# Hybrid attention and delta-rule layer: 32x32 block inverses by substitution on GpSimd, two chunks at a time

## The reference, cut to what matters

```
lower = jnp.where(strict, jnp.einsum('bhncd,bhnsd->bhncs', k_beta, k) * decay, 0.0)
system = lower + jnp.eye(C, dtype=lower.dtype)
sol = lax.linalg.triangular_solve(system, rhs, left_side=True, lower=True)
a_qk = jnp.where(causal, jnp.einsum('bhncd,bhnsd->bhncs', q, k) * decay, 0.0)
def step(state, inp):
    v_new = u_c - jnp.einsum('bhcd,bhde->bhce', w_c, state)
    o_c = jnp.einsum('bhcd,bhde->bhce', q_c, state) + jnp.einsum('bhcs,bhse->bhce', a_c, v_new)
    state = state * jnp.exp(gl_c)[..., None, None] + jnp.einsum('bhcd,bhce->bhde', kd_c, v_new)
```

## Time and profile before

| what | us |
|---|---|
| median of 3 executions (2544.60 to 2553.95) | 2550.47 |
| the profiled execution | 2535.64 |
| its span | 2533.9 |
| TensorE busy | 2312.9 (91%) |
| VectorE busy | 1082.2 (43%) |
| ScalarE busy | 906.8 (36%) |
| GpSimd busy | 390.6 (15%) |

### The profile page before, as it was taken

How to read it: one execution, slowest core, us unless ns; L and a number is a source line. 1 busy time by engine, 2 the same in 40 slices (tenths; PEclk the granted TensorE clock), 3 DMA queues, 4 the chain that set the end, 5 groups by cost and what they waited for, 6 DMA issues and landing times. The chain is left out here.

```text
span 2533.9 us, 47637 instructions
## 1 busy us (share of the span) xinstructions
PE 2312.9 (91%) x17494; PEld 1329.8 (52%) x17495; DVE 1082.2 (43%) x2488; ACT 906.8 (36%) x2283; POOL 390.6 (15%) x630
## 2 busy tenths in 40 slices
PE   6999999999779999999999997799966999999990
PEld 2545545455356666666666665355534444444440
DVE  2434333343346666666666565133344222222223
ACT  2263462633635555555555544011110010101112
POOL 1000000000111001000000000233221222222224
PEclk9999999999979999999999999899987999999995
DMA  9212121111263213211222103733311879999787
GB/s 335 73 67 76 51 82 44 55 63 36 89 163 106 76 54 95 86 58 63 71 72 80 41 27 155 270 113 129 125 67 50 245 215 309 270 324 301 217 237 290
DMA packets 187895, 334.49 MB, mean 132 GB/s; under 512 B 19723, under 2 KB 119718, under 8 KB 184502
## 3 DMA queue, kind: packets, MB, share of 16 engines
q1 hardware_dynamic: 173878, 281.51, 32.8%
q0 software_dynamic: 13824, 50.34, 8.2%
HBM read 242.36 MB, written 89.44 MB: 131 GB/s over the span
## 5 line engine op out<-in xcount | busy, mean ns | idle before, releaser
L708 PE MATMUL pV<-mod_rows_then_work,w_in_sb 128*128 128x512 f32 x768 | 340.7, 597 | 4.4 <-DMA w_in_sb<-in_w_in_dram 4.4
L2079 PE MATMUL hidden_ps<-w,keys_values_then_all 128*128 x752 | 331.5, 594 | 1.2 <-SPq L1951 1.2
L1147 ACT ACTIVATE probs<-scores,neg_max 128x512 f32<-128x512 f32 (+3 forms) x320 | 199.6, 624 | 332.0 <-DVE neg_max L1276 218.5
L1430 PE MATMUL scores<-keys_values_then_all,queries 96*128 96x512 f32 (+3 forms) x640 | 303.5, 557 | 7.6 <-DMA keys_values_then_all<-kp_d 7.6
L2079 PEld LDWEIGHTS hidden_ps<-w,keys_values_then_all 128*128 128x128 f32 x752 | 143.2, 191 | 181.7 <-issue 181.7
L708 PEld LDWEIGHTS pV<-mod_rows_then_work,w_in_sb 128*128 128x128 f32 x768 | 144.7, 191 | 177.5 <-issue 176.8
L1728 PE MATMUL out_ps<-keys_values_then_all 128*128 128x512 f32 x512 | 226.2, 600 | 2.5 <-ACT keys_values_then_all L1593 2.5
L1435 PE MATMUL bank<-ident,probs 128*128 128x128 f32 x1088 | 183.4, 284 | 1.5 <-ACT probs L1147 1.2
L2009 ACT ACTIVATE keys_values_then_all<-hidden_ps 128x256 f32<-128x256 f32 x47 | 18.0, 384 | 455.7 <-PE hidden_ps L2079 455.7
L1276 DVE TENSOR_REDUCE neg_max<-scores 128x1 f32<-128x512 f32 x192 | 132.2, 688 | 111.5 <-PE scores L1430 110.4
L1447 PE MATMUL outT_ps<-probs_T,keys_values_then_all 128*64 128x128 f32 x2176 | 156.3, 282 | 22.2 <-issue 18.5
(11 more groups left out here) (367 smaller groups left out, 3337.9 us busy)
## 6 DMA issues: line engine op xcount, KB each, us to landing
w<-in_w_dram SPq DMA_DIRECT2D x64, 1024.0 KB, 10.0
w_sb<-in_w_dram SPq DMA_DIRECT2D x32, 1024.0 KB, 14.2
w_mod_rows<-in_w_mod_dram SPq DMA_DIRECT2D x16, 1024.0 KB, 4.8
kqv<-qkv_d SPq DMA_DIRECT2D x16, 768.0 KB, 4.3
mod_rows_then_work<-in_w_mod_dram SPq DMA_DIRECT2D x4, 2048.0 KB, 15.0
x_in<-in_x_dram SPq DMA_DIRECT2D x16, 512.0 KB, 3.5
qkv_d<-l_out SPq DMA_DIRECT2D x32, 256.0 KB, 2.3
keys_values_then_all<-y_d SPq DMA_DIRECT2D x16, 512.0 KB, 5.0
```

The source lines that it names most:

```text
L708: last = pe.matmul(pV[n % 2][:], win[:, k, QKV0 + c * P:QKV0 + (c + 1) * P], hT[:, s % 2, k, :], start=(k == 0), stop=(k == ND - 1))
L1147: act.activation(prob[:, e, 0:w].rearrange("p t k -> p (t k)"), pS[e][:, 0:w * P], ACT.Exp, scale=-1.0, bias=nmin[:, i % 2, h, b:b + 1], a ...
L1430: pe.matmul(pS[e][:, 0:w * P], qT[:, i % 2, slot(h)], kT[:, 4 * b:4 * b + w, slot(h), :], start=True, stop=True).then_inc(s_ready, 1)
L2079: last = pe.matmul(pH[par][:], xT[par][:, k], m.w13[:, ds(slot, 1), k].rearrange("p s n -> p (s n)"), start=(k == 0), stop=(k == ND - 1))
```

## The change

The 32x32 inverses leave TensorE. GpSimd computes them by substitution, for two chunks at once: 2 chunks x 4 blocks x 4 heads are 32 matrices, one on each of partitions 96 to 127 (a free corner of the key-value buffer). For column j it multiplies the entries below j with the solved row j (an outer product) and subtracts it from the rows below: 31 columns, two instructions each, each waiting for the one ahead. The 16 pieces (`I`, two columns each) are spread over two turns. LB loads the blocks of one chunk, four DMAs on GpSimd's own queue; after the last piece GpSimd makes a transposed copy and stores both to DRAM by its queue.

For that K and KA now run for chunk c+4 in turn c (before c+1), on a second buffer of keys and queries (`kk`); their results go to DRAM (`store_products`) and come back with the inverses in a new step L (`load_inverses`: seven block loads, `lt` and `at`, all on SP) at the end of turn c for chunk c+2. W0, U0, KB, D and the doubling levels are gone; the two joining levels are now Y and WU 1 and 2. The gate buffers are two instead of three.

```diff
-LVB, BL = 5, 32
+BL = 32
+AHEAD, BATCH = 4, 2
+PIECES = 16
...
+def spread(steps, between):
+
+    if not between:
+        return steps
+    cut = [k * len(steps) // len(between) for k in range(len(between) + 1)]
+    return [x for k, piece in enumerate(between) for x in [piece] + steps[cut[k]:cut[k + 1]]]
...
-    for c in range(-2, NT):
-        n, d = c + 1, c + 2
-        prep, rec = 0 <= n < NT, c >= 0
...
+    for c in range(-AHEAD, NT):
+        n, a, d = c + 1, c + AHEAD, c + AHEAD + 1
+        first, prep, rec = a < NT, 0 <= n < NT, c >= 0
+        g, half = (c + 3) // BATCH, (c + 3) % BATCH
+        pieces = [(0.8 if c < 0 else 0.0, ("I", g, k)) for k in range(half * PIECES // 2, (half + 1) * PIECES // 2)]
+        pieces *= 0 <= g < NT // BATCH
+        lead = [(1.0, ("K", a)), (0.5, ("KA", a))] * first
+        lead += [(0.45, ("VT", c)), (0.45, ("KD", c)), (1.0, ("KS", c)), (0.7, ("QS", c))] * rec
+        lead += [(0.0, ("LB", a))] * (first and not half)
+        lead += [(0.85, ("TR", c))] * rec
+        body = [(0.8, ("Y", n, 1))] * prep
+        body += [(0.85, ("DS", c))] * rec
+        body += [(0.9, ("WU", n, 1))] * prep
+        tail = [(0.85, ("AV", c))] * rec
+        tail += [(0.8, ("Y", n, 2))] * prep
+        tail += [(0.0, ("O1", c))] * rec
+        late = [(0.9, ("M", k)) for k in MOD_AT.get(c, ())[:-1]]
+        late += [(0.5, ("WU", n, 2))] * prep
+        late += [(0.0, ("G", d))] * (d < NT)
+        late += [(0.9, ("M", k)) for k in MOD_AT.get(c, ())[-1:]]
+        late += [(0.0, ("O2", c))] * rec
+        mid = [(0.0, ("IS", g))] * (half and len(pieces) > 0) + [(0.0, ("LB", a))] * (half and first)
+        if half:
+            turn = spread(lead + body, pieces) + tail + mid + late
+        else:
+            turn = lead + spread(body + tail + late, pieces)
+        turn += [(0.0, ("L", c + 2))] * (0 <= c + 2 < NT)
+        steps += turn
+    order = [("G", 0), ("K", 0), ("KA", 0), ("LB", 0), ("G", 1), ("S", 0, 0), ("X", 0, 0), ("S", 0, 1), ("X", 0, 1)]
...
-    NLV = 6
+    NLV = 2
...
-        lt = sb("A_transposed", [P, GH, P])
-        ltb, xt = sb("A_blocks", [P, GH, BL]), sb("X_transposed", [P, LVB, GH, BL])
+        lt, lt_new, at_new = (sb(n, [P, GH, P]) for n in ("A_transposed", "A_ahead", "qk_ahead"))
+        corner = m.kv[QK:P, 0:4096]
+        Ab = corner[:, 0:BL * BL].rearrange("p (j i) -> p j i", j=BL)
+        both_T = corner[:, BL * BL:3 * BL * BL]
+        Tb, Ub = (both_T[:, k * BL * BL:(k + 1) * BL * BL].rearrange("p (i j) -> p i j", i=BL) for k in range(2))
+        outer = corner[:, 3 * BL * BL:3 * BL * BL + BL * BL // 4]
...
+            def store_products(c):
+                wait(lt_ready, c + 1)
+                sp.dma_start(m.a_d[c * P:(c + 1) * P, :], lt_new[:].rearrange("p h i -> p (h i)")).then_inc(lt_stored, 16)
+                wait(at_ready, c + 1)
+                sp.dma_start(m.qk_d[c * P:(c + 1) * P, :], at_new[:].rearrange("p h i -> p (h i)")).then_inc(at_stored, 16)
+
+            def load_inverses(c):
+                wait(inv_stored, 16 * (c // BATCH + 1))
+                wait(xw_ready, NLV * c)
+                wait(tr_ready, c - 1)
+                if c == 0:
+                    sp.wait_ge(zero_made, 3)
+                for q in range(4):
+                    rows = m.inv_d[(c * 4 + q) * GH:(c * 4 + q + 1) * GH, :].rearrange("h (k i j) -> i h k j", k=2, i=BL)
+                    sp.dma_start(U[c % 2][quarter[q], :, quarter[q]], rows[:, :, 1]).then_inc(blocks_back, 16)
+                    if q < 3:
+                        dst = Wh[quarter[q], :, quarter[q]] if q < 2 else Wb[quarter[q]]
+                        sp.dma_start(dst, rows[:, :, 0]).then_inc(blocks_back, 16)
+                sp.dma_start(lt[:].rearrange("p h i -> p (h i)"), m.a_d[c * P:(c + 1) * P, :]).then_inc(lt_loaded, 16)
+                wait(av_ready, c - 1)
+                wait(at_stored, 16 * (c + 1))
+                sp.dma_start(at[c % 2][:].rearrange("p h i -> p (h i)"), m.qk_d[c * P:(c + 1) * P, :]).then_inc(at_loaded[c % 2], 16)
...
             load_k(0)
+            load_kq(1)
+            load_g(1)
             load_v(0)
+            load_kk(2)
             load_q(1)
-            load_g(1)
-            load_kq(1)
             load_gate(0)
...
-                if kind == "K" and n + 2 < NT:
-                    wait(em_ready, n + 1)
-                    load_g(n + 2)
+                if kind == "K":
+                    if 2 <= n < NT - 1:
+                        wait(kk_ready, n + 1)
+                        load_kk(n + 1)
+                    if n + 2 < NT:
+                        wait(em_ready, n + 1)
+                        load_g(n + 2)
+                elif kind == "KA":
+                    store_products(n)
+                elif kind == "L":
+                    load_inverses(n)
...
+            def then(ins):
+                done[0] += 1
+                ins.then_inc(inv_step, 1)
+                pool.wait_ge(inv_step, done[0])
+
+            def load_blocks(c):
+                wait(lt_stored, 16 * (c + 1))
+                for q in range(4):
+                    at_row = (c % BATCH * 4 + q) * GH
+                    pool.dma_start(Ab[at_row:at_row + GH], m.a_d[c * P + BL * q:c * P + BL * (q + 1), :].rearrange(
+                        "j (h r i) -> h r j i", h=GH, r=4)[:, q]).then_inc(block_loaded, 16)
+
+            def invert(g, piece):
+                n = P - QK
+                wait(em_ready, made["G"])
+                wait(o_pow, 2 * made["O1"])
+                wait(a_pow, 2 * made["A"])
+                if piece == 0:
...
+                    then(pool.memset(both_T[:, 0:BL * BL], 0.0))
+                    then(pool.memset(both_T[:, 0:BL * BL:BL + 1], 1.0))
+                    pool.wait_ge(block_loaded, 16 * 4 * BATCH * (g + 1))
+                for j in range(piece * BL // PIECES, (piece + 1) * BL // PIECES):
+                    below, upto = BL - 1 - j, j + 1
+                    if below:
+                        prod = outer[:, 0:below * upto].rearrange("p (i c) -> p i c", i=below)
+                        then(pool.tensor_tensor(prod, Ab[:, j, j + 1:].unsqueeze(2).to_broadcast([n, below, upto]),
+                                                Tb[:, j:j + 1, 0:upto].to_broadcast([n, below, upto]), ALU.mult))
+                        then(pool.tensor_tensor(Tb[:, j + 1:, 0:upto], Tb[:, j + 1:, 0:upto], prod, ALU.subtract))
+                if piece == PIECES - 1:
+                    pool.tensor_copy(Ub, Tb.rearrange("p i j -> p j i")).then_inc(inv_ready, 1)
+                    wait(inv_ready, g + 1)
+                    pool.dma_start(m.inv_d[g * (P - QK):(g + 1) * (P - QK), :], both_T).then_inc(inv_stored, 16)
...
+                if kind in made:
+                    made[kind] += 1
                 if kind == "G":
                     wait(exp_ready, n + 1)
                     wait(at_ready, n)
                     pool.tensor_tensor(em[:], dm[:, n % 2], m.upper[:].unsqueeze(1).to_broadcast([P, GH, P]), ALU.mult).then_inc(em_ready, 1)
-                elif kind == "KB":
-                    wait(ltb_ready, n + 1)
-                    wait(xw_ready, NLV * (n - 1) + LVB - 1)
-                    pool.tensor_tensor(xt[:, 1:], ltb[:].unsqueeze(1).to_broadcast([P, LVB - 1, GH, BL]),
-                                       mask_b[:, 1:].unsqueeze(2).to_broadcast([P, LVB - 1, GH, BL]), ALU.mult).then_inc(xt_ready, 1)
+                elif kind == "LB":
+                    load_blocks(n)
+                elif kind == "I":
+                    invert(n, step[2])
+                elif kind == "K":
...
-                    wait(xw_ready, n * NLV)
+                    wait(lt_stored, 16 * n)
                     both = [bank[b] for b in at_bank[step]]
                     for h in range(GH):
-                        last = dve.scalar_tensor_tensor(out=lt[:, h], in0=both[h // 2][:, (h % 2) * 2], scalar=beta[:, cols(n, h)],
+                        last = dve.scalar_tensor_tensor(out=lt_new[:, h], in0=both[h // 2][:, (h % 2) * 2], scalar=beta[:, cols(n, h)],
                                                         in1=em[:, h], op0=ALU.mult, op1=ALU.mult)
                     last.then_inc(lt_ready, 1)
...
-                    wait(av_ready, n - 1)
+                    wait(at_stored, 16 * n)
                     both = [bank[b] for b in at_bank[("K", n)]]
                     for g in range(2):
-                        last = dve.tensor_tensor(at[n % 2][:, g * 2:g * 2 + 2], both[g][:].rearrange("p (h two) i -> p h two i", two=2)[:, :, 1],
+                        last = dve.tensor_tensor(at_new[:, g * 2:g * 2 + 2], both[g][:].rearrange("p (h two) i -> p h two i", two=2)[:, :, 1],
                                                  em[:, g * 2:g * 2 + 2], ALU.mult)
                     last.then_inc(at_ready, 1)
...
-                    wait(kq_loaded[n % 2], 16 * (n // 2 + 1))
+                    both = kk if n >= 2 else kq[n]
```

(21 more changed lines are left out.)

159 lines of the change are left out of this document (42 added, 117 removed).

## The result

| | before | after |
|---|---|---|
| median, us | 2547.53 (4 runs, 2543.08 to 2553.95) | 2476.32 (4 runs, 2475.15 to 2480.07) |
| the profiled execution | 2535.64 | 2475.72 |
| its span | 2533.9 | 2474.0 |

The ratio is 0.9721, 95% interval 0.9695 to 0.9747: 2.8% faster. Forecast were 2498.5 us, range 2468 to 2546. The sign, the place and the range hold; the gain is 71 us by the medians and 60 by the profiled executions, where the sum gave 52. The profiled execution of before lay near the low end of its own spread (all runs of it beside the experiments: 2533 to 2554), that of after close to its median.

What follows compares the result with a forecast made beforehand. TensorE, 91% busy, was taken to bound the kernel. -73.9 (products) - 3 (idle) + 19 (start) + 6 (stalls) = -52 us: 2483.6 for the profiled execution, plus 14.8 gives a 2498.5 us median; range 2468 to 2546.

Steps and rivals of the forecast that it cites:

- What goes: Mixing stage, TensorE: the removed W0, Y and WU products, priced from each step's start to its successor's, save 73.9 us.
- My bound of 81.4: Upper bound in us on the saving from the removed TensorE products: row sums 124.9 less one overlapping WU line, 43.5.
- GpSimd's price: Substitution on GpSimd: 39.8 us per two-chunk inversion, mean 0.64 us an instruction; 43.4 with clearing and copy; 1.1 per DMA issue.
- The placing: GpSimd's in-order queue in the mixing stage: margins of 4.4 and 3.4 us ahead of G; 6 us of new stalls.
- The G behind the pieces: The danger on GpSimd: the decay mask step G queued behind substitution pieces, delaying VectorE's K, score reductions and TensorE.
- the laying of GpSimd's turn: A timed 42 us mid-stage turn placing A, pieces, O1 and G on GpSimd; G(8) ends at 41, wanted at 45.4.
- The start: Stage start: 11 us idle TensorE behind LB(0) and G(1), 5 for clock, 3 at first inversion: +19 us, bounds 5 and 35.
- The clock: Stage start: with the pause, TensorE's clock stays at its lower level for some 10 us more work, +5 us.
- GpSimd sets the pace: Rival: dearer substitution instructions ahead of G and O1 make it slower; 2629 us at a mean of 1.1 us; chance 0.16.
- No room: Rival: 0.8 us instructions or 1.6 us block loads use up the margins, start costs 35: about 2538 us; chance 0.14.
- The port: Rival: VectorE's two-input gate product blocks against GpSimd's SBUF reads, 19 us if all reach TensorE, 2518 us; chance 0.1.
- The start costs nothing: Rival: at the stage's start the stores overtake the loads, so no start loss: 2478 us; chance 0.1.

Runs made afterwards that it cites:

- two here: On the changed kernel, each alone: AS put back in front of its row's last values step (2476.09 us); G(1) and chunk 0's products store issued earlier (2479.96 us).
- the edit that took their common cover away: The changed kernel with the powers of O1 and A on ScalarE instead of GpSimd: 2453.05 us, stage 22.5 us shorter; with the other two edits 2436.44 us.

## Why the prediction was right, and where it was not

- **What goes, 73.9 us: too small.** Its own part was nearly right: 76.2 over all 144 steps, idle left out (82.4 with the idle inside them and ahead of their successors). What I left out is what the steps do to their neighbours, about 0.1 us each. The busy time fell by 90.2, though after ran 16 us more at the lower clock, which hides up to 8 us more; without columns it fell by 101.6. My bound of 81.4 held for the products and not for the busy time.
- **GpSimd's price: right.** Instructions of 32 partitions and short runs cost what the wide ones predict: 605 and 697 ns at 240 elements (forecast 0.69), gap 0.09. A block-load issue took 0.72 us instead of 1.1, the copy 1.96 instead of 2.4. The first inversion ended with its store at 792.9, forecast 789.
- **The placing: danger named, mechanism incomplete.** "The G behind the pieces" is what happened: VectorE waited for the mask in every second chunk from 849 to 1204, 13.0 us in all beside the start's 13.3. That is under 2 us a chunk, as forecast, but it left TensorE idle for 15.2 where the sum has 6. The step that failed is the laying of GpSimd's turn ("O1 until 34; pieces 5 and 6 and G(8) until 41"). It gives O1 and A their 2 us and lets the pieces run on. But a power holds GpSimd until its input comes, 8.4 us ahead of O1 at 930, so the pieces pile up between it and G; and it holds ScalarE when it comes late. The runs put 22.5 us there, and 31 for all columns, against 6 + 3.
- **The start, 19 us: events right, size not shown.** LB(0) was issued by 723.4 (728), G(1) ended at 724.7 (729), the first V came at 727.2 (732), TensorE idle 11.7 (11). The clock, +5 in the sum, had already risen at 711.7 (before at 719.2), fell to 0.50 at 718.5 inside the pause and rose at 732.2, after 5.0 us of work: about 2.5 us lost, against 7.5 us of earlier rise. Early, G(1) moved the first V forward but not the end.
- **The end, 0: missed.** AS moved behind the last V of its row, its store behind SP's loads of the next stage: 6.5 us.
- **The sum.** By the runs: without columns the stage is 94.6 us shorter than before, the start's pause included; the columns give 30.6 back, the end 6.5, and the stages behind are 2.4 shorter: 60. The forecast had 61 for the first (73.9 + 3 - 16), 9 for the second (6 + 3), nothing for the third. So the removal was too small, the columns too cheap by 22 and the end missed, and the start cheaper by an amount that stays open. That these errors cancelled to 8 us on the profiled execution is luck; the rest of the 22 us on the median is my adding 14.8 for an execution that was merely one of the quicker ones of its kernel.
- **The rivals.** *GpSimd sets the pace*: not at x = 0, though its sign, a wait for decay in every second chunk, is there at 1.3 to 4.2 us; its slope held when I added 0.29 us. *No room*: no. *The port*: exists, at most 4 us of stage where I had 19. *The start costs nothing*: no, yet its 2478 us is the number that came.

## What to carry to other kernels

Before work is given to an engine with a low busy share, list what else that engine computes for others, and look at its waits: in an in-order queue the free time in front of a wait can't be used, and each small instruction that others wait for gets the new work's length added. Move those small instructions away first. And price what goes with its neighbours: removing 76 us of small products took 90 us of busy time off. And an edit that gives nothing alone may be covered by another wait: two here gave nothing one by one, and 17 us behind the edit that took their common cover away.
